# Seven half-size products for 18 tile pairs of a float32 projection, with the index stage placed later and a 512-wide second output

## The reference, cut to what matters

```python
h = rmsnorm(x, g_pre)
z = einsum('btd,de->bte', h, w_in)
q, k, v, ga, qi, ki, wi, bg, cg, hc, gb = split(z, offsets)
# indexer: scores per query and key, the best 256 keys are kept (132 of 528 for the streams)
iscore = sum_h(relu(qi_h . ki) * wi_h); sel = top_k(iscore)
attn = softmax(q . k[sel]) . v[sel]
u = cg * hc; conv = bg * (w0*u[t-2] + w1*u[t-1] + w2*u[t])
z = concat([attn * silu(ga), conv * silu(gb)])
y = x + rmsnorm(z . w_out, g_post)
```

## Time and profile before

| | |
|---|---|
| runs shown | 2342.75, 2345.25, 2349.07 us, median 2345.25 us |
| the profiled execution | 2350.3 us by its own time, its span 2348.5 us |
| PE busy | 2263.6 us, 96% of the span |
| VectorE, ScalarE, GpSimd busy | 993.3, 718.8, 758.2 us |
| mean granted clock of TensorE | 0.990 |

### The profile page before, as it was taken

The page is one execution under the profiler, slowest core; times in us unless marked ns, Lnnn a source line. Parts: engine busy times, 40 slices in busy tenths (PEclk is TensorE's granted clock), DMA queues, the critical chain, the costliest instruction groups (busy, mean ns, idle before and its releaser), DMA issues.

```text
span 2348.5 us, 33638 instructions
## 1 busy us (share of the span) xinstructions
PE 2263.6 (96%) x14005; PEld 2082.7 (89%) x14005; DVE 993.3 (42%) x1703; ACT 718.8 (31%) x1089; POOL 758.2 (32%) x328
## 2 busy tenths in 40 slices
PE   5999999999999999999998999999999999999996
PEld 5999998999999999877787888887877799999996
DVE  4000006891261112255213969797885634303212
ACT  5121123312211124343333342424223633324221
POOL 4333332232233333322222434342432222233442
PEclk9999999999999999999999999999999999999998
DMA  6433342343222244454654433334342624137644
GB/s 163 118 89 106 102 111 65 88 86 86 65 80 84 81 121 136 116 149 131 169 151 130 124 108 103 98 103 110 85 124 81 192 78 127 52 108 239 241 145 170
DMA packets 423244, 276.86 MB, mean 118 GB/s; under 512 B 55395, under 2 KB 401827, under 8 KB 421045
## 3 DMA queue, kind: packets, MB, share of 16 engines
q1 hardware_dynamic: 423092, 274.71, 40.5%
HBM read 230.58 MB, written 44.09 MB: 117 GB/s over the span
## 4 chain that ended last, share of the span: by engine, by line
PE 84%; DVE 9%; issue 2%; ACT 2%; DMA 2%; SPq 1%; DVEq 0%; ACTq 0%
PE ps L891 57%; PE ps L921 16%; PE ps L948 4%; PE ps L848 3%; PE ps L999 2%; DVE isc L1542 2%; DVE top L1541 1%; DVE act_lo L1355 1%; PE ps L1071 1%; DVE isc L1529 1%; DVE F L1580 1%; PE ps L982 1%; DMA conv<-z_mix 1%; DVE F L1604 1%; DMA w_raw<-in_w_in 0%
## 5 line engine op out<-in xcount | busy, mean ns | idle before, releaser
L820 POOL TENSOR_TENSOR w_lo<-w_raw,w_hi 128x1024 fp32r<-128x1024 f32 x308 | 743.8, 2415 | 1537.2 <-ACT w_hi L1102 1537.2
L891 PE MATMUL ps<-act_hi,w_hi 128*128 128x320 f32 (+1 forms) x2928 | 839.2, 340 | 6.6 <-DVE act_lo L1355 4.1
L891 PE MATMUL ps<-act_lo,w_hi 128*128 128x320 f32 (+1 forms) x2928 | 830.5, 337 | 0.0
L891 PE MATMUL ps<-act_hi,w_lo 128*128 128x320 f32 (+1 forms) x2928 | 830.4, 337 | 0.0
L891 PEld LDWEIGHTS ps<-act_hi,w_hi 128*128 128x128 f32 x2928 | 511.9, 189 | 54.1 <-issue 14.4
L1102 ACT ACTIVATE w_hi<-w_raw 128x1024 fp32r<-128x1024 f32 x308 | 326.1, 1059 | 751.6 <-PE ps L891 533.0
L891 PEld LDWEIGHTS ps<-act_hi,w_lo 128*128 128x128 f32 x2928 | 512.3, 188 | 39.5
L891 PEld LDWEIGHTS ps<-act_lo,w_hi 128*128 128x128 f32 x2928 | 512.8, 189 | 35.4
L921 PE MATMUL ps<-w_hi,act_hi 128*128 128x256 f32 x1152 | 326.6, 283 | 1.4 <-ACTq L1169 1.0
L921 PE MATMUL ps<-w_hi,act_lo 128*128 128x256 f32 x1152 | 325.8, 283 | 0.0
L921 PE MATMUL ps<-w_lo,act_hi 128*128 128x256 f32 x1152 | 325.7, 283 | 0.0
(11 more groups left out here) (150 smaller groups left out, 1521.7 us busy)
## 6 DMA issues: line engine op xcount, KB each, us to landing
w_raw<-in_w_in SPq DMA_DIRECT2D x244, 512.0 KB, 3.9
w_raw<-in_w_out SPq DMA_DIRECT2D x64, 512.0 KB, 4.3
qraw<-z_qi SPq DMA_DIRECT2D x24, 256.0 KB, 4.7
fin_x<-in_x_prompt SPq DMA_DIRECT2D x6, 1024.0 KB, 8.5
conv<-z_mix SPq DMA_DIRECT2D x16, 320.0 KB, 4.0
z_og<-ev SPq DMA_DIRECT2D x8, 640.0 KB, 4.1
fin_o<-z_og SPq DMA_DIRECT2D x5, 1024.0 KB, 5.5
out<-fin_o SPq DMA_DIRECT2D x10, 512.0 KB, 5.2
```

Source lines behind the costliest of these rows:

```text
L820: nc.gpsimd.tensor_tensor(w_lo[:, r], w_raw[:, r], w_hi[:, r].bitcast(F32), ALU.subtract).then_inc(sem_w_lo, 1)
L891: last = nc.tensor.matmul(ps[:, bank + x, 0:w], wt[:, r, k % 8], a[:, k, w * x:w * (x + 1)], start=(k == 0 and wt is w_hi and a is act_hi) ...
```

## The change

For 18 pairs of neighbouring tiles of A (tiles 5 to 40: the qi and q tiles, and (cg, hc), (bg, gb) of five of the eight convolution blocks) the 2x2 block product (two halves of the contraction, two tiles, two halves of the columns) is done by seven products of half size in place of eight. VectorE makes four mixed activations once (mixed_raw and mixed_low; ScalarE makes their hi in mixed_high) and four combinations of the weights for each pair (weights_combined). A pair has 14 half chunks of 128x512: ScalarE copies each to sh_hi (pair_high), GpSimd subtracts to sh_lo (pair_low), PE does 12 matmuls of 320 columns with each (pair_products). ScalarE and VectorE add the products up in ev (pair_first, pair_sum), and VectorE does with the result what was done with the tiles (pair_done). Weights are loaded in quarters of 512 KB into five places (rb), which lie over the old ring. The mixed activations lie over the buffers of the attention, so the index stage and its loads wait for the last product (sem_sg).

The index stage of A starts at tile 42.25, streams first, with an end of NP + 1; the list of NX and those behind it are as they were. B's output projection moves 512 columns at a time in 4 column blocks (out_gemm_wide, quad_out, quad_squares), with eight banks in two sets of four. g_pre is loaded a second time behind the pairs, since the last mixed part lies over it.

```diff
-OUTP = [("o", i, 2 * P * (i // 2)) for i in range(KT)]
+QW, QUADS = 4 * P, KT // 4
+OUTP = {"A": [("o", i, OW * (i // 2)) for i in range(KT)], "B": [("o", i, QW * (i // 4)) for i in range(KT)]}
+FIRST_PAIRED, PAIRS_W = 5, 18
+PRODUCT_BANK = (2, 3, 2, 0, 1, 0, 1)
...
-    place([(("CHUNKS", 0), 1), (("CHUNKS", 1), 1), (("IK", "A"), 2)]
-          + index_steps(2, US_A) + index_steps(3, US_A) + stream_index_steps(), 22, NP - 7)
+    place([(("CHUNKS", 0), 1), (("CHUNKS", 1), 1)] + stream_index_steps() + [(("IK", "A"), 2)]
+          + index_steps(2, US_A) + index_steps(3, US_A), LAST_PAIRED + W["after"], NP + 1)
     place([(("NX", i), 8) for i in range(5, 9)], NP - 6, NP - 1)
...
+            def pair_loads(p):
+                a, b, c, d, e = raw_places(p)
+                sp.wait_ge(sem_s_cmb, 4 * p + 4)
+                    load_quarter(p + 1, 0, 0, a)
+                sp.wait_ge(sem_s_lo, HALVES * p + 8)
+                    load_quarter(p + 1, 0, 1, b)
+                sp.wait_ge(sem_s_lo, HALVES * p + 10)
+                    load_quarter(p + 1, 1, 1, e)
+                    sp.wait_ge(sem_s_lo, HALVES * p + 12)
+                    load_quarter(p + 1, 1, 0, c)
...
+            def pair_low(p):
+                for half in range(HALVES):
+                    q = HALVES * p + half
+                    x = product_raw(p, half // 2)[:, 4 * (half % 2):4 * (half % 2) + 4]
+                    pool.wait_ge(sem_s_hi, q + 1)
+                    nc.gpsimd.tensor_tensor(sh_lo[q % 4], x, sh_hi[q % 4].bitcast(F32), ALU.subtract
+                                            ).then_inc(sem_s_lo, 1)
...
+            def pair_products(p):
+                for j in range(PRODUCTS):
...
+                    if j == 2:
+                        pe.wait_ge(sem_s_first, 2 * p + 1)
+                    if j in (5, 6):
+                        pe.wait_ge(sem_s_sum, 5 * p + j - 3)
+                    for c in range(2):
+                        q = HALVES * p + 2 * j + c
+                        pe.wait_ge(sem_s_lo, q + 1)
+                        for k in range(4):
+                            for i, (w, a) in enumerate(((sh_hi, hi), (sh_hi, lo), (sh_lo, hi))):
+                                last = nc.tensor.matmul(ps[:, bank, 0:T2], w[q % 4][:, k], a[:, 4 * c + k, :],
...
+            def pair_high(p):
...
+                        if half == 0:
+                            if j in (0, 2, 5):
+                                act.wait_ge(sem_rb_ld[place], 16 * raw_loads(p, place))
+                            else:
+                                act.wait_ge(sem_s_cmb, 4 * p + {1: 3, 3: 2, 4: 1, 6: 4}[j])
+                            act.wait_ge(sem_sg, q - 3)
+                        copy(sh_hi[q % 4], product_raw(p, j)[:, 4 * half:4 * half + 4]).then_inc(sem_s_hi, 1)
...
+            def weights_combined(p, i):
+                if i == 0:
+                    nc.vector.tensor_tensor(e, b, c, ALU.add).then_inc(sem_s_cmb, 1)
+                elif i == 1:
+                    nc.vector.tensor_tensor(b, a, b, ALU.subtract).then_inc(sem_s_cmb, 1)
+                elif i == 2:
+                    dve.wait_ge(sem_s_lo, HALVES * p + 2)
+                    nc.vector.tensor_tensor(a, e, a, ALU.subtract).then_inc(sem_s_cmb, 1)
+                else:
+                    dve.wait_ge(sem_s_lo, HALVES * p + 6)
+                    nc.vector.tensor_tensor(d, d, a, ALU.subtract).then_inc(sem_s_cmb, 1)
...
+            def pair_done(p):
+                if kind == "cg":
+                    nc.vector.tensor_tensor(c_up[:, 2:514], one[:, 0:512], two[:, 0:512], ALU.mult)
+                    link(nc.vector.tensor_tensor(c_us[:, :, 2:18], one[:, 512:640].rearrange("p (b t) -> p b t", b=NB),
+                                                 two[:, 512:640].rearrange("p (b t) -> p b t", b=NB), ALU.mult))
+                    conv_sums("A", c)
+                elif kind == "bg":
+                    link(nc.vector.tensor_tensor(c_y, one, c_y, ALU.mult))
+                    nc.vector.tensor_tensor(two, c_y, two, ALU.mult).then_inc(sem_ev_rdy[e % 2], 1)
...
+                    p = (n - FIRST_PAIRED) // 2
+                    if p:
+                        pair_sum(p - 1, 4)
+                        pair_done(p - 1)
+                    weights_combined(p, 3)
+                    for i in range(3):
+                        pair_sum(p, i)
+                    if p + 1 < PAIRS_W:
+                        weights_combined(p + 1, 0)
+                        weights_combined(p + 1, 1)
+                    pair_sum(p, 3)
+                    if p + 1 < PAIRS_W:
+                        weights_combined(p + 1, 2)
...
+                for i in range(4):
+                    nc.vector.tensor_tensor(o_nat[:, i, c:c + QW], quad_place(quad, i), gbc[:, c:c + QW], ALU.mult
+                                            ).then_inc(sem_o_cp, 1)
```

More of the change, by code:

```diff
@@ L92, with paired, chunk, chunk_tile @@
 LAST_HC = ("B", "hc", 7)
+FIRST_PAIRED, PAIRS_W = 5, 18
+LAST_PAIRED = FIRST_PAIRED + 2 * PAIRS_W
+T2 = T_A // 2
+PRODUCTS = 7
+PRODUCT_BANK = (2, 3, 2, 0, 1, 0, 1)
+HALVES = 2 * PRODUCTS
+SPLITS = HALVES * PAIRS_W
+def paired(n):
+    return FIRST_PAIRED <= n < LAST_PAIRED
+def chunk(h):
+    return h if h < 2 * FIRST_PAIRED else h - 4 * PAIRS_W
+def chunk_tile(i):
+    return i if i < 2 * FIRST_PAIRED else i + 4 * PAIRS_W
+def raw_places(p):
+    a, b, c, d, e = 1, 2, 0, 3, 4
+    for _ in range(p):
+        c, d, e = e, c, d
+    return a, b, c, d, e
 EV = {}
@@ L312 @@
 QI_ALL = sum(1 for s in ORDER if s[0] == "QI")
+PT_ALL = sum(1 for s in ORDER if s[0] == "PT")
 PT_A = sum(1 for s in ORDER if s[0] == "PT" and s[1] < 4)
@@ L430, in build @@
         o_stat = [stat[:, 24 + 5 * i:29 + 5 * i] for i in range(4)]
+        mixed = ExitStack()
+        t_part = [sb(f"t_part{i}", [P, KT // 2, T2], F32R, mixed) for i in range(7)]
+        mixed.close()
+        t_hi = [t[:] for t in t_part[0:4]]
+        t_lo = [t[:] for t in t_part[4:7] + [t_last]]
+        t_raw = conv[:, 0:KT // 2 * T2].rearrange("p (k t) -> p k t", k=KT // 2)
         attention = ExitStack()
@@ L498, in residual, with raw_loads, product_raw, quarter @@
             return (fin_x if i < 7 else fin_o)[:, i % 2]
+        def raw_loads(p, place):
+            return sum(1 for i in range(p + 1) for x in raw_places(i)[0:4] if x == place)
+        def product_raw(p, j):
+            a, b, c, d, e = raw_places(p)
+            return rb[(a, a, d, b, e, c, d)[j]]
+        def quarter(a, k, t):
+            return a[:, 8 * k:8 * k + 8, T2 * t:T2 * t + T2]
+        def pair_slots(p):
+            n = FIRST_PAIRED + 2 * p
+            kind, index = TILES[n][1:3]
+            if n in EV:
+                return EV[n] % 2, EV[n + 1] % 2
+            f = EV[tile_number("A", "gb", index)] % 2
+            return (f, 1 - f) if kind == "cg" else (1 - f, f)
+        def slot_spills(n, slot):
+            return sum(1 for t, e in EV.items() if t < n and e % 2 == slot and TILES[t][1] in SPILLED)
+        def pair_ev(p, i):
+            u = ev[:, pair_slots(p)[i]]
+            return u[:, 0:T2], u[:, T2:T_A]
         def ev_free(e):
@@ L900, in out_gemm @@
             def out_gemm(n, s):
                 group, _, index, _ = TILES[n]
-                tiles, pair = TT[group], index // 2 + PAIRS * (group == "B")
+                if group == "B":
+                    out_gemm_wide(n, s)
+                    return
+                tiles, pair = TT[group], index // 2
                 quarter, h = 2 * (index % 2) + s // 4, 2 * n + s // 4
                 if s % 4 == 0:
-                    pe.wait_ge(sem_w_lo, h + 1)
+                    pe.wait_ge(sem_w_lo, chunk(h) + 1)
@@ L1181, in product_squares @@
             def product_squares(n):
                 group, _, index, _ = TILES[n]
[L1184 removed]
+                if group == "B":
+                    if index % 4 == 3:
+                        quad_squares(n)
+                    return
+                pair = index // 2
                 act.wait_ge(sem_nat_sq, bank_use(pair, 0))
```

393 lines of the change are left out of this document (334 added, 59 removed).

## The result

The changed kernel takes **2312.64 us** (median of four runs, 2311.22 to 2312.83) against 2346.74 for the kernel before (four runs, 2342.75 to 2349.07): a ratio of 0.9854, 95% interval [0.9839, 0.9869], 34 us faster. The profiled execution took 2312.46 us with a span of 2310.6.

What follows compares the result with a forecast made beforehand. PE was taken to bound the kernel, busy for 96% of the span. The terms summed to -23.3 us, giving 2327 from the profiled execution and 2322 us from the median; range 2296 to 2350, the forecast's own 2310 to 2336.

Steps and rivals of the forecast that it cites:

- Matmuls, q pairs, sh_lo, B's output: Pairs' matmuls 63.4 us less, q pairs at PE's 24.64, half subtraction 1.30 us, B's wider output 9.9 less, its end 1 more.
- Entry and exit: Start and end of the paired tiles: 4 us for the first copy and combination chain, 2 us for the first plain chunk.
- Conv pairs: Convolution pairs, POOL and DVE times added at the port: (cg, hc) pairs over 27 us, losing 14; (bg, gb) pairs losing 10.
- late combinations: (bg, gb) pairs: the previous pair's taps wait behind POOL and delay the next weight combinations, 2 us each, 10 in all.
- the paragraph on queues: Weight loads of the pairs: SP waits for POOL, with only spills behind it and quarters landing in 3.9 us; cost 0.
- the port doesn't bind: Rival for the pairs: quick half subtraction or overlapping waits, so the 24 us of port loss stay saved, 2298 us; chance 0.18.
- Rows of x: Tile 60: B's four rows of x fall into slot 479 and stall PE's transposes, with late loads and half clock; 16 us.
- B's lists: B's step lists shift by 17.4 slots and nine steps pile into slot 999, 3 us (0 to 8).
- The index stage: Rest of A's index stage, moved beside the (cg, hc) to ga tiles: same widths, order within blocks and PE work; 0 us.
- slow POOL: Rival: POOL's half subtraction isn't nearly half; decides from 1.44 us, and at 1.55 the time is 2373 us; chance 0.10.
- rows hidden: Rival: ACT and DVE run far enough ahead to hide the four rows of x, 2306 us; chance 0.15.
- rows double: Rival: the four rows of x cost double, with late loads and half clock, 2338 us; chance 0.12.

Runs made afterwards that it cites:

- e_taps: e_late with the convolution's work reordered on DVE, the fourth weight combination ahead of the taps: 2302.33 us, ratio 0.9811.
- e_notaps: Changed kernel without the taps and sums of group A's five paired convolution blocks, so its conv is not the reference's: 2305.92 us, ratio 0.9831.
- e_halves: Changed kernel with each half subtraction of POOL in the pairs done as two of 256 elements: 2321.04 us, ratio 0.9892.
- e_spread: Changed kernel with the four rows of x at slots 432, 440, 448 and 466, not counted by the cursor: 2303.93 us, ratio 0.9815.
- e_late: Changed kernel with the four rows of x at slots 460, 463, 466 and 469, not counted by the cursor: 2295.19 us, ratio 0.9791.
- e_order: e_late with the last nine TK steps of block 3 moved to slots 482 to 495: 2298.23 us, ratio 0.9801.
- e_noclip: Changed kernel with B's index and softmax list ending two tiles later, spreading the nine steps piled in slot 999: 2307.36 us, ratio 0.9836.
- b_shift: Kernel before, without pairs, with only the list cursor set to 524.7 as in the changed kernel: 2362.81 us, ratio 1.0078.
- e_inlist: Changed kernel with the four rows of x counted inside the index stage's list, ahead of block 3's TK steps: 2318.24 us, ratio 0.9889.

## Why the prediction held, and which of its terms did not

The direction, the range and the forecast's own range (2310 to 2336) held 2312.6. The profile fell by 37.8 us where the sum said 23.3 (34.1 by the medians). Two terms were far off, 15.7 us too high and 14.2 too low, and nearly cancel, which is luck: without the second the time would have been near 2298, below the forecast's own range. What is left of the difference are the rows of x (4.7), the index stage (5.6) and the first tiles (some 2).

- **Matmuls, q pairs, sh_lo, B's output.** Right: 24.63 us for a pair, 1.30 us for a half subtraction, -10.7 for B's output and +0.95 behind it, where I had 24.64, 1.30, -9.9 and +1. The Trainium skill, GPSIMD Engine Reference, section 3.1, has 4497 ns for 2048, which with the row of 1024 had made an estimate of 1.37; the measurement lies at what this kernel's own rows gave.
- **Entry and exit**, 4 + 2: measured 4.5 (tile 4 17.5 us against 14.6, the first pair 26.2) and 1.7.
- **Conv pairs, 14 + 10: mis-sized, measured 8.3.** The failed step is "I add both up for each pair" as a loss of each pair. The product and the taps of a (cg, hc) pair run beside the (bg, gb) pair behind it, which by the sum had 18.2 + 4.9 + 4.3 = 27.4 us at the port and took 24.87. Two neighbours have 52.1 us by the sum; they took 51.2, and 50.6 in e_taps with the same work. So the 14 us did not come, nor the sign "(cg, hc) over 27". What came is the sentence behind it, on late combinations: 2 us were taken for each of five (bg, gb) pairs, and 1.7 to 2.1 us came in the four pairs behind one (behind the fifth stands a plain tile). The place was missed, since PE waits one pair later, for a load that SP issues late: the paragraph on queues had SP wait for POOL, while pair_loads waits first for DVE's fourth combination, behind taps that POOL stretches from 2.9 to 8.8 us. The rival "the port doesn't bind" was right for 15.7 of its 24 us; that it isn't right for the rest is shown by e_notaps, where the taps' 6.7 us go.
- **The port's rule.** DVE's combination stretches from 1.22 to 2.0 to 2.3 us beside POOL, and POOL's pieces stretch beside DVE (e_halves), as an exclusive hold would have it. The Trainium skill, SBUF — State Buffer, section "SBUF: two separate sides", has the port locked for a whole instruction. The stretched operations agree with it (the last section has the numbers); that each engine's lengths may therefore be added up to a time of the pair does not follow, as the conv pairs show.
- **Rows of x, 16 (9 to 20): right in place and mechanism, measured 11.3.** Rows follow at 4.0 us, not 4.3; no wait for POOL came, since POOL was idle, and the loads were in time, so the stall is 7.4 us in place of 12.5 + 2. The clock costs 3.8 in place of 1.5. Elsewhere the rows cost as much: in e_spread, e_late and e_order they met DVE, which has 158 of 192 us to do from tile 50 to 60 in e_late, at tile 56, 60 or 63.
- **B's lists, 3 (0 to 8): failed, measured 17.2.** "B's lists shift by 17.4 slots" was given a price for the pile in slot 999 alone, 3 us (3.5 to 5.6 by e_noclip), and none for the shift. b_shift makes the whole loss from the shift and its pile in the old kernel. I had no row for it and gave it no bound; in e_inlist, with these lists one or two slots and the softmax of A 8 slots later, two tiles cost 30 more. Which steps meet which tiles is shown by PE's idle time; why each single wait grows was not taken apart.
- **The index stage, 0: measured -5.6.** Its side steps made tiles 5 to 59 longer by 55.8 us over the plain 14.08 a tile, and by 50.2 in the changed kernel's tiles 41 to 59. Its order is another (streams first); no run separates the reason.

Of the rivals, slow POOL is out (1.30 us), rows hidden and rows double are out (11.3). Two sums of the prediction do not follow from its terms: for slow POOL the lengths it names make 252 p + 118 and the other terms +16, so it decides from 1.48 (1.44 only with the 10 us of late combinations counted too); and 4.4 us for "the taps' own length" is nearly the whole 4.3 us that a (cg, hc) pair adds, of which the taps are 2.9. Neither changes the outcome.

## What to carry to other kernels

A list of steps that is laid out by a cursor makes every later stage part of an edit: price the shift of each list behind the change, not only the place where lists collide, and try it by itself in the old kernel (one line here, 18 us). Do not take the summed lengths of two engines at a shared port for a time: here they were 0.9 to 5 us over what two pairs took. Follow the longest chain through the load queue: a load that waits for a late engine is a wait that no occupancy shows. Before a stage is moved beside another, add up the engine that both need: four rows of 4 us cost some 9 to 14 us in each of four places behind a late index stage, and six pairs fewer were faster than 18.
